# LoRA's first layer as products with h and with h shifted, and r's first projection ahead of LoRA's second layer

## What is computed

```python
prev = concatenate([shift_prev, h[:, :-1]])
xx = prev - h
xr, xw, xk, xv, xa, xg = [h + xx * mu[j] for j in range(6)]
r = xr @ w_r;  k = xk @ w_k;  v = xv @ w_v
wlog = -softplus(-(w0 + tanh(xw @ w1) @ w2)) - 0.5      # w1: D x 64, w2: 64 x D
a = sigmoid(a0 + (xa @ a1) @ a2)                        # a1: D x 64, a2: 64 x D
g = sigmoid(xg @ g1) @ g2                               # g1: D x 128, g2: 128 x D
```

## Time and profile before

| | |
|---|---|
| median of 3 runs | 3569.94 us (3566.77 to 3571.16) |
| the profiled execution's own time | 3569.57 us |
| its span (first to last instruction) | 3567.4 us |
| TensorE busy | 3098.2 us, 87% of the span, 32142 matmuls |
| VectorE, ScalarE, GpSimd busy | 1824.9, 1229.6, 963.5 us |
| mean granted TensorE clock | 0.956 of 2.4 GHz |

### The profile page before, as it was taken

The page is one execution under the profiler, slowest core; times in us unless marked ns, Lnnn a source line. Parts: engine busy times, 40 slices in busy tenths (PEclk is TensorE's granted clock), DMA queues, the critical chain, the costliest instruction groups (busy, mean ns, idle before and its releaser), DMA issues.

```text
span 3567.4 us, 73896 instructions
## 1 busy us (share of the span) xinstructions
PE 3098.2 (87%) x32142; PEld 2968.9 (83%) x32142; DVE 1824.9 (51%) x1785; ACT 1229.6 (34%) x1418; POOL 963.5 (27%) x524
## 2 busy tenths in 40 slices
PE   5788679999999996589986888878779999999996
PEld 4788579999999995589985766666779999999996
DVE  4656674455445457512205666666355445454455
ACT  4332232222122224643315666766322112221222
POOL 2121122232222222423312333332322222222221
PEclk9999889999999998889998999999989999999998
DMA  2111001111111110142221212121201111111111
GB/s 93 33 39 33 24 24 48 42 42 47 41 41 47 42 42 24 56 162 91 85 101 38 61 51 62 51 55 36 96 27 46 42 42 47 41 42 47 41 42 63
DMA packets 92396, 186.18 MB, mean 52 GB/s; under 512 B 33536, under 2 KB 56576, under 8 KB 92160
## 3 DMA queue, kind: packets, MB, share of 16 engines
q1 hardware_dynamic: 85248, 155.85, 14.1%
q10 hardware_dynamic: 6912, 26.84, 1.9%
HBM read 146.12 MB, written 36.53 MB: 51 GB/s over the span
## 4 chain that ended last, share of the span: by engine, by line
PE 70%; DVE 18%; ACT 6%; issue 2%; POOL 2%; DMA 1%; ACTq 0%; DVEq 0%; SPq 0%; POOLq 0%
PE PS L961 61%; PE PS L1093 8%; DVE T L1331 4%; ACT T L457 2%; DVE T L1321 2%; DVE X L1321 2%; DVE T L1444 2%; DVE HL L1321 1%; DVE G L1321 1%; DVE B L1321 1%; DVE M L1336 1%; DVE AR L1331 1%; DVE SS L1326 1%; ACT HH L457 1%; ACT X L457 1%
## 5 line engine op out<-in xcount | busy, mean ns | idle before, releaser
L961 PE MATMUL PS<-HH,WH 128*128 128x364 f32 x3528 | 790.8, 333 | 122.6 <-POOL HL L812 78.4
L812 POOL TENSOR_TENSOR WL<-RAW,WH 128x1024 fp32r<-128x1024 f32 x206 | 498.4, 2419 | 1450.4 <-ACT WH L457 1446.2
L961 PE MATMUL PS<-HL,WH 128*128 128x364 f32 x3528 | 787.8, 332 | 0.0
L961 PE MATMUL PS<-HH,WL 128*128 128x364 f32 x3528 | 786.6, 332 | 0.0
L961 PEld LDWEIGHTS PS<-HH,WH 128*128 128x128 f32 x3528 | 617.9, 191 | 141.9 <-issue 72.8
L961 PEld LDWEIGHTS PS<-HH,WL 128*128 128x128 f32 x3528 | 620.7, 190 | 0.0
L961 PEld LDWEIGHTS PS<-HL,WH 128*128 128x128 f32 x3528 | 620.2, 191 | 0.0
L1331 DVE SCALAR_TENSOR_TENSOR T<-T,FP 128x1092 f32<-128x1092 f32 x192 | 456.0, 2375 | 6.8
L1321 DVE TENSOR_TENSOR X<-PS,X 128x1092 f32<-128x1092 f32 x224 | 290.2, 1296 | 283.5 <-PE PS L961 279.8
L961 PE MATMUL PS<-PH,WH 128*128 128x364 f32 x1344 | 304.3, 336 | 80.9 <-DVE X L1321 38.6
L457 ACT ACTIVATE WH<-RAW 128x1024 fp32r<-128x1024 f32 x206 | 218.6, 1061 | 435.4 <-PE PS L961 417.4
(11 more groups left out here) (134 smaller groups left out, 3507.3 us busy)
## 6 DMA issues: line engine op xcount, KB each, us to landing
RAW<-weights SPq DMA_DIRECT2D x206, 512.0 KB, 3.6
scratch<-T ACTq DMA_DIRECT2D x32, 546.0 KB, 2.9
scratch<-SR ACTq DMA_DIRECT2D x16, 546.0 KB, 2.9
X<-xT SPq DMA_DIRECT2D x8, 546.0 KB, 9.4
yT<-T SPq DMA_DIRECT2D x8, 546.0 KB, 2.8
T<-scratch_m SPq DMA_DIRECT2D x8, 512.0 KB, 4.1
LW<-scratch SPq DMA_DIRECT2D x16, 192.0 KB, 2.5
KK<-scratch SPq DMA_DIRECT2D x16, 192.0 KB, 2.6
```

Of the source, the lines that this page charges most:

```text
L812: pool.tensor_tensor(out, full, hi, ALU.subtract).then_inc(*t.made(event))
L961: mm = pe.matmul(acc[:, j, :], a, b[:, j * CW:(j + 1) * CW], start=(i == 0 and q == 0), stop=(i == len(blocks) - 1 and q == 2))
```

## The change

LoRA's first layer no longer uses mixed inputs. As (h + (prev - h) mu) W = h (W - mu W) + prev (mu W), it multiplies h with one set of weights and h shifted with another, for w1|a1 (one tile, mu1 for its 64 columns of w1 and mu4 for those of a1) and for g1 (mu5). GpSimd makes mu W and W - mu W in the kernel, behind the last convolution of layer 0's ConvFFN; their high parts for the shifted set are ScalarE's, ahead of its squares. The sums run over k, and within k over both products, 36 matmuls for each k and 288 in all, where 216 were. h itself is split into high and low parts (`HS`, `HSL`, rows of 1094 columns that lie where `HH` and `HL` do; h is read from column 2, h shifted from column 1). r's mix is then written over them, behind TensorE's use of each k, and the first of r's eight products runs between the two layers of LoRA. The second layer keeps 24 products of 9 matmuls, but those of w2 and a2 have 64 rows of weights instead of 128 half of zeros. The weights come to 4 tiles instead of 6 ahead of r, k and v. r, k and v keep 24 products. `MIXES` is `[0, 2, 3]`.

```diff
         HH = at("HH", [KT, COLS], h_at, F32R)
-        HL = at("HL", [KT, COLS], h_at + KT * COLS * 4, F32R)
+        HL = at("HL", [KT, COLS], l_at, F32R)
+        HS = at("HS", [KT, COLS + 2], h_at, F32R)
+        HSL = at("HSL", [KT, COLS + 2], l_at, F32R)
...
@@ ScalarE
+            for q in range(2):
+                act.wait_ge(*t.next("mu_w"))
+                run(TR[:, 6 + q, 0:D], T[:, q, 0:D], ACT.Copy, "sh_hi")
             norm(m, added(m - KT), n, "two")
...
-            act.wait_ge(*t.at("hf", KT + 2))
+            for k in range(KT):
+                act.wait_ge(*t.at("hf", 2 * k + 3))
+                run(HS[:, k, :], HF[:, k, PAD - 2:ROW], ACT.Copy, "h_hi")
             mix_half()
             mix_half()
-            for k in range(KT):
+            for k in range(KT - 1):
                 mix_hi(None, k)
-            for k in range(KT):
-                mix_hi(m, k)
             lora, lora_g = T[:, 6, 0:COLS], T[:, 7, 0:COLS]
...
+            half_acc = lambda h: ACC[m % 2][HALF[h]]
+            run(row3(lora)[HALF[0]], half_acc(0), ACT.Tanh, "lora")
+            run(row3(lora)[HALF[1]], half_acc(1), ACT.Copy, f"taken{m % 2}", n=m // 2 + 1)
+            mix_hi(m + 1, KT - 1)
+            evacuate(m + 1, row3(lora_g), ACT.Sigmoid)
+            run(TR[:, 0, 0:COLS], lora, ACT.Copy, "lora_hi")
             w_hi(n + 1, m + 2)
...
+            spill(m, 3, 0, ACT.Copy)
+            m += 1
+            w_hi(n, m)
+            n += 1
+            act.wait_ge(*t.at("lora_lo", 2))
             for j in range(3):
                 for f in range(KT):
...
-                    if j < 2 and f % 2:
-                        mix_hi(m0 + 2, (KT * j + f) // 2)
                     m += 1
@@ GpSimd
+            pool.wait_ge(*t.at("conv", KT + 2 * FT))
+            for q, parts in ((0, ((1, 0, CHUNK), (4, CHUNK, P))), (1, ((5, 0, P),))):
+                pool.wait_ge(*t.at(f"dma_w{q}", W_PROJ // 2 + 1))
+                for j, a, z in parts:
+                    mu = V[:, VAT[f"mu{j}"]:VAT[f"mu{j}"] + KT].unsqueeze(2).to_broadcast([P, KT, z - a])
+                    if t.latest:
+                        pool.wait_ge(*t.own())
+                    pool.tensor_tensor(by_mu(T[:, q, 0:D])[:, :, a:z], RAW[q][:, :, a:z], mu, ALU.mult).then_inc(*t.made("mu_part"))
+                pool.wait_ge(*t.own())
+                pool.tensor_tensor(RAW[q][:, :, :], RAW[q][:, :, :], by_mu(T[:, q, 0:D]), ALU.subtract).then_inc(*t.made("mu_w"))
+            for q in range(2):
+                rest(TR[:, q, 0:D], T[:, q, 0:D], TR[:, 6 + q, 0:D], "sh_hi", "sh_lo")
+            w_lo(2)
...
+                    rest(HSL[:, k, :], HF[:, k, PAD - 2:ROW], HS[:, k, :], "h_hi", "h_lo")
@@ TensorE
+            for k in range(KT):
+                pe.wait_ge(*t.next("h_lo1" if k % 2 else "h_lo"))
+                for q in range(2):
+                    acc = ACC[(m + q) % 2]
+                    s, sh, sl = (n + q) % 2, TR[:, 6 + q, k * P:(k + 1) * P], TR[:, q, k * P:(k + 1) * P]
+                    for i, (w, x, c) in enumerate(((WH[s][:, k, :], HS, 2), (WH[s][:, k, :], HSL, 2), (WL[s][:, k, :], HS, 2),
+                                                   (sh, HS, 1), (sh, HSL, 1), (sl, HS, 1))):
+                        for j in range(CH):
+                            mm = pe.matmul(acc[:, j, :], w, x[:, k, j * CW + c:(j + 1) * CW + c],
+                                           start=(k == 0 and i == 0), stop=(k == KT - 1 and i == 5))
...
+            up(m, n, fresh=True)
+            m, n = m + 1, n + 1
+            for rows, r in ((HALF[0], 0), (HALF[1], 0), (slice(0, P), 2)):
+                if rows != HALF[1]:
+                    pe.wait_ge(*t.next("w_lo"))
+                    pe.wait_ge(*t.next("lora_lo"))
+                s = n % 2
+                for f in range(KT):
+                    split_product(m, [(WH[s][rows, f, :], WL[s][rows, f, :], TR[rows, r, 0:COLS], TR[rows, r + 1, 0:COLS],
+                                       None, None)])
+                    m += 1
@@ VectorE
-            h_rows("mix1", 0, "hf")
...
+            for k in range(KT):
+                stt(HF[:, k, PAD:ROW], X[:, k, :], vec("mix1", k), T[:, 2, 0:COLS], ALU.mult, ALU.mult, "hf")
+                copy(HF[:, k, PAD + HIST:PAD + SAMPLE], vec("shift", k), "hf")
+                if k and k % 2 == 0:
+                    rest_of(k - 1)
+            rest_of(KT - 1)
```

More of the change, by code:

```diff
@@ L688, in _ @@
                         spill(m, j, f, ACT.Copy)
-                    if j < 2 and f % 2:
-                        mix_hi(m0 + 2, (KT * j + f) // 2)
                     m += 1
-                w_hi(n, m)
-                n += 1
+                if j:
+                    w_hi(n, m)
+                    n += 1
             for j in range(3, 6):
-                for f in range(KT):
+                for f in range(j == 3, KT):
                     if f == KT - 1 and j < 5:
@@ L867, in ffn @@
                 w_lo(2)
-                w_lo(2)
             for k in range(KT):
@@ L872, in _, with by_mu @@
             ffn()
-            assert n == W_PROJ + 2
-            for k in range(2 * KT):
-                h_lo(k % KT, mix_row(k))
-            w_lo()
-            for k in range(KT):
-                h_lo(k, mix_row(2 * KT + k))
+            assert n == W_PROJ
+            def by_mu(t_):
+                return t_.rearrange("p (k c) -> p k c", k=KT)
+            pool.wait_ge(*t.at("conv", KT + 2 * FT))
[11 more added lines that the diff above has]
+            w_lo(2)
+            for k in range(KT):
+                if k % 2:
+                    t.n["h_hi"] += 1
+                else:
+                    rest(HSL[:, k, :], HF[:, k, PAD - 2:ROW], HS[:, k, :], "h_hi", "h_lo")
+            for k in range(KT):
+                h_lo(k, mix_row(k))
             w_lo()
@@ L1047, in _ @@
             m += 1
-            for q in range(3):
-                up(m + q, n + q, fresh=True, release=True)
-            m, n = m + 3, n + 3
-            for j in range(3):
-                pe.wait_ge(*t.next("w_lo"))
-                pe.wait_ge(*t.at("lora_lo", 2 if j == 2 else 1))
-                s, r = n % 2, 2 if j == 2 else 0
-                for f in range(KT):
-                    split_product(m, [(WH[s][:, f, :], WL[s][:, f, :], TR[:, r, 0:COLS], TR[:, r + 1, 0:COLS], None, None)])
-                    m += 1
-                n += 1
@@ L1060, in _ @@
-            with pe.Fori(0, 3) as turn:
-                t.enter(turn, dict(w_lo=KT, h_lo=KT // 2, h_lo1=KT // 2, acc_ready=KT, taken0=KT // 2, taken1=KT // 2, h_used=KT - 1))
-                for f in range(KT):
-                    up(m + f, n + f, fresh=(f == 0), release=(f == KT - 1))
-                t.leave(3)
-            m, n = m + 3 * KT, n + 3 * KT
+            for q in range(2):
+                pe.wait_ge(*t.next("w_lo"))
+                pe.wait_ge(*t.next("sh_lo"))
+                pe.wait_ge(*t.at(f"taken{(m + q) % 2}", (m + q) // 2))
@@ new lines, in _ @@
+            for k in range(KT):
+                pe.wait_ge(*t.next("h_lo1" if k % 2 else "h_lo"))
+                for q in range(2):
+                    acc = ACC[(m + q) % 2]
[5 more added lines that the diff above has]
+                                           start=(k == 0 and i == 0), stop=(k == KT - 1 and i == 5))
+                    if k == KT - 1:
+                        mm.then_inc(*t.made("acc_ready"))
+                if k < KT - 1:
+                    mm.then_inc(*t.made("h_used"))
@@ new lines, in _ @@
+            m, n = m + 2, n + 2
+            up(m, n, fresh=True)
+            m, n = m + 1, n + 1
+            for rows, r in ((HALF[0], 0), (HALF[1], 0), (slice(0, P), 2)):
+                if rows != HALF[1]:
+                    pe.wait_ge(*t.next("w_lo"))
+                    pe.wait_ge(*t.next("lora_lo"))
[4 more added lines that the diff above has]
+                    m += 1
+                if rows != HALF[0]:
+                    n += 1
@@ L1066, in _ @@
+            for j in range(3):
+                for f in range(j == 0, KT):
+                    up(m, n, fresh=(f == 0), release=(j < 2 and f == KT - 1))
+                    m, n = m + 1, n + 1
             assert (m, n) == (M_OUT, W_OUT)
```

103 lines of the change are left out of this document (42 added, 61 removed).

## The result

The changed kernel takes 3529.69 us (median of 4 runs, 3526.47 to 3531.96) against 3570.55 (3566.77 to 3573.07) for the kernel before, run beside it: ratio 0.9887, 95% interval 0.9871 to 0.9902. It is 41 us faster, where 67 were forecast, and the time sits at the upper end of the range of 3489 to 3530. The profiled execution took 3526.47 us, with a span of 3524.7.

The account below looks back on a forecast made before the run. Bound by TensorE nearly everywhere, except LoRA's layers, paced by mixes and by ScalarE's spills. r's second product at 1507.0 instead of 1574.0 gains 67.0 us, 3569.57 to 3502.6, plus 0.4: 3503 us, range 3489 to 3530.

Parts of the forecast that it names:

- Step 1: End of layer 0: the weights' preparation delays the squares and the norm's product to 1386.0, 8.6 us lost.
- My bound of 4.9 above: End of layer 0: 4.9 us more lost, 14 in all, if broadcast multiplications run at half rate.
- Step 2: Norm to first matmul: TensorE starts at 1398.8 instead of 1402.63, since no mix stands in between.
- Step 3: Joint first layer: 288 matmuls take 48.1 us plus 2.3 cold, ending at 1449.2 where it was 1481.0.
- Rivals B and C: First layer fed no faster, 3531 us, chance 0.08; off-start HS reads at plain fp32 price, 3639 us, chance 0.04.
- Step 4: r's first product between LoRA's layers: a 0.6 us gap, then 12.0 us, ending at 1461.8.
- r's eight stay, off the path: Joint first layer: r's eight mix tiles follow h's use, 6.4 us of work per two tiles against 12.0.
- Step 5: LoRA's second layer: ScalarE's spills at 1.64 us set the pace; r's second product starts at 1507.0.
- term for landings: Second layer: spills land a little late for buffer reuse, 3 us added; bounds 0 and 9.
- Rival A: Second layer at half clock through small waits between products: 23 us more, 3526 us, chance 0.10.
- The sum: r's second product at 1507.0 instead of 1574.0, gain 67.0 us; everything behind keeps counts and waits: 3503 us.
- upper bounds of steps 1 and 5: 14 us lost at layer 0's end, and 9 us added for spills in LoRA's second layer.

Follow-up runs that it names:

- e8: Changed kernel with four scratch rows instead of two for r's mix and three tiles made ahead: 3519.34 us, ratio to the kernel before 0.9862.
- e1: Changed kernel with all 128 rows again for w2 and a2 in LoRA's second layer (results not the reference's): ratio to the kernel before 0.9862.
- e5: Changed kernel with 226 fulfilled waits on TensorE ahead of the recurrence, putting the last ConvFFN's loop at instruction place 227: 3521.04 us, ratio 0.9866.
- e6: Kernel before with 286 fulfilled waits on TensorE, putting the last ConvFFN's loop at instruction place 114: 3573.17 us against 3568.17, ratio 1.0012.
- e10: Changed kernel with r's first product behind LoRA's second layer again: 3534.78 us, ratio to the kernel before 0.9908.
- e11: Changed kernel with r's mix three tiles ahead, shifted split behind the squares, 128 half-zero rows for w2 and a2, and loop-placing waits: 3504.18 us, ratio 0.9819.
- e3: Changed kernel with four scratch rows instead of two for r's mix and four tiles made ahead: 3526.48 us, ratio to the kernel before 0.9884.
- e7: Kernel before with 64 rows instead of 128 half of zeros for w2's and a2's products: 3571.25 us, ratio 1.0008.
- e2: Changed kernel with w2's and a2's products interleaved matmul by matmul into both accumulators: 3532.27 us, ratio to the kernel before 0.9896.

## Why the prediction was right and wrong

**Step 1, right.** 8.6 us lost were forecast, 1385.24 - 1377.41 = 7.8 came (7.6 by the averages of seven and three profiles), by the mechanism that I named: GpSimd's chain to `mu_w`, ScalarE waiting ahead of its squares. The multiplication with a broadcast operand, for which I had no row, takes 1.90 us, less than the subtraction. My bound of 4.9 above was needless. That most of the loss was a matter of order I saw (everything queued behind is late) and did not question.

**Step 2, right** (1398.03 for 1398.8). **Step 3, right** (ends at 1449.1 for 1449.2, no wait, 0.167 us per matmul on `HS` from both columns). Rivals B and C are out: the table shows 51.07 of 51.1 us busy, and reads that start 4 or 8 bytes off the rows' usual start cost nothing.

**Step 4, wrong by 6.8 us:** a stand of 5.4 instead of 0.6, and 14.0 us cold instead of 12.0. What failed is a clause of step 3, "r's eight stay, off the path", with "12.84 / 2 = 6.4 us of work for two". The price came from the earlier trace rows, where the mixes of LoRA have four scratch rows (`i % 4` in `mix_row`). r's mix has two (`4 + i % 2`), in both kernels; before, it lay between the spills of the second layer, and I took the price of the one for the other. The chain is then 9.1 us for two tiles. It stays inside the 12.0 us per two tiles that TensorE's release would allow, and yet it is late, because it starts only when h is all made (1417.7) and GpSimd has four of its eight tiles: 1421.99 + 3 x 9.16 = 1449.47 for the last. e8 shows it: with only these rows, their number ahead and their waits changed, the stand is 0.67 us and r's product takes 12.2.

**Step 5, wrong by 9.7 us:** 54.9 instead of 45.2. The mechanism that I had (spills, two weights' high parts, landings) is there, in e1: 49.2 us at a clock of 0.93. Its term for landings was undersized by 4: in e1 ScalarE waits 4.8 + 3.1 us for spills to land, where I had added 3. The other 5.7 us are the half clock. Rival A gave the right sign and a price for it, 23 us on 24 products at half clock; the price was itself 3 too high, since 65.4 us have to be set against the 45.2 of the whole layer and not against the 42 from its first spill on. Some 14 of the 24 ran so, and part of what they cost took the place of waits for spills (3.0 + 1.2 us in the changed kernel, 4.8 + 3.1 in e1). But its reason was wrong, and so was my argument against it: I answered that TensorE would be busy 1.5 of 1.64 us, and it was busier than that, all of the time from 1475.4 to 1507.9, at 1.2 GHz. The 64 rows stood in the diff; I had counted them as matmuls like the others.

**The sum, wrong by 7 us more:** "what follows keeps counts and waits". Counts it keeps, but not its place in the instruction stream. e5 and e6 give 5.4 and 3.9 us for that. Some 2 us more lie in the rest of r, k and v (a wait at a reload is 2.90 instead of 1.90 us); that stretch takes 299.2 to 300.6 us in five profiles with this code (after, e1, e8, e10, e11) and 298.5 before. The cause was not tested.

**The range.** That the time lies inside it, at its upper end, is luck. The range had room there for the half clock, or for the upper bounds of steps 1 and 5, and these two alone come to 3503 + 5.4 + 6 = 3514, not 3530. The time got there by 6.8, 9.7 and some 7 us in four places, of which only the half clock and the landings had a price.

Steps 4 and 5 and the sum have one thing in common: a price was carried over from the kernel before to work that now has another form or place (a mix with two rows, matmuls of 64 rows, a loop with another number of instructions ahead of it).

## What to carry to other kernels

When work is taken off the critical path, cost the chain that is left at its new number of buffers: a producer that waits for the buffer it has just handed on runs all engines in turn, and one buffer more than the distance ahead takes that away (9.1 us to some 5 for two tiles, e3 against e8). Don't trim a matmul's rows for their own sake: nine matmuls at full clock took 1.6 us with 64 rows and 1.5 with 128 (e1), and the 64-row form of these fp32r matmuls cost 5.7 us of clock here. When a program gets longer or shorter, look at the instruction queue and at waits for "issue" in loops far behind the edit, and measure a change of 0.1 to 0.2% with the loop put back where it was.

## What the hardware showed beyond what I expected

- TensorE with fp32r matmuls of 64 rows and 364 columns stays at 1.2 GHz once it is there, though it is busy 32.50 of 32.50 us (after; also e7, e8, e10); the same with 128 rows comes back to 2.4 GHz within 6 us, also behind a wait of 2 us (after, e1). Half of those rows may be zeros (e11). It is no rule for every matmul of 64 rows: the recurrence is made almost wholly of plain fp32 ones of 64 by 64, many of them in turn on both halves of the rows, and there the clock is 0.98 from 1900 to 2000 us with TensorE busy 80% (after). Which of type, columns and halves makes the difference no run shows.
- Two 64-row matmuls on opposite halves of the array run side by side: twelve in 1.27 us at full clock, as six alone (e2).
- The place of a long loop in TensorE's instructions costs 4 to 5 us over the last ConvFFN, 0.8 against 0.2 MB of instructions (e5, e6).
- GpSimd's multiplication of 1024 elements with an operand broadcast over groups of 128 takes 1.90 us, its subtraction of two plain operands 2.40 (after); whether the operand or the operation makes the difference no run shows.
